# Mean of squares of a latent: one TensorE product of a summed tile instead of one per tile, issued two outputs later

## The chip, the cores and the metric

One core of one Trainium2 chip runs the whole program. TensorE (PE) multiplies matrices into PSUM banks, VectorE (DVE) and ScalarE (ACT) do elementwise work, GpSimd (POOL) a little more, and SyncE's queue (SP) issues nearly all transfers. The engines run side by side and are ordered by semaphores. The metric is the device time of one execution in microseconds; smaller is better.

## The reference, cut to what matters

```python
proj = h @ w_in                                  # 2064 rows (16 meta + 2048), width 1024
c_q, c_kv, k_rope, z = jnp.split(proj, ...)      # 384, 256, 32, 1024 columns
q = (rms_norm(c_q, q_norm_g) @ w_uq)
c_kv = rms_norm(c_kv, kv_norm_g)
k_nope = (c_kv @ w_uk); v = (c_kv @ w_uv)
# rms_norm: x * rsqrt(mean(square(x), -1) + 1e-6) * g
```

Attention, an output projection, a layer norm and a second, convolutional layer follow; the change doesn't touch them.

## The kernel before

Everything is held transposed: a latent is stored as tiles of 128 latent columns (on the partitions) by tokens. The first stage, `stage_p`, cuts the 2064 tokens into 8 chunks of 258 and makes each latent chunk by chunk. Latents 0 to 7 are the key-value ones (2 tiles of 128, `KKV`), 8 to 15 the query ones (3 tiles, `KQ`). Matrix products of float32 data are done as three products of a high and a low part (lines 43 to 45, `split_matmul`).

The order of the stage is the list `STEPS_P`: p0, p1, o0, p2, o1, p3, o2, ... p15, o14, o15, then eight z steps. Step p *g* projects chunk *g* (`project`, three tiles of 24 matmuls each into banks 0 to 2). Step o *g* makes the outputs of latent *g* (`make`): for a key-value latent 8 key tiles k0 to k7 (6 matmuls of 258 columns each) and 4 or 6 halves of value tiles v0, v1, ... (6 matmuls of 512 columns); for a query latent 12 tiles (9 matmuls each), every third of which, n = 2, 5, 8, 11, is a rotary one. Outputs go to banks 4 to 7 in turn, so output *r* waits until output *r*-4 was taken from its bank. Takers (`take`): VectorE takes the even key tiles and the rotary ones, ScalarE the rest. A key latent's step therefore has k0, k2, k4, k6 on VectorE and k1, k3, k5, k7 and all values on ScalarE.

Between the outputs of step o *g* the chain of latent *g*+1 is run, spread over three engines by hand:

- ScalarE copies the projected tiles to `craw`, VectorE squares them into `sq` (`squares`, line 588).
- TensorE's `mean_squares` (line 492) multiplies a matrix that holds 1/256 or 1/384 everywhere by each tile of `sq` in plain float32 and accumulates in bank 3. Each such product stands in the trace as two matmuls.
- VectorE adds epsilon (`mean_taken`, 614), ScalarE takes the root (390), VectorE inverts (`inverse`, 618), refines (`newton`, 621 to 624) and scales (`normalise`, 629); ScalarE rounds to the high part (394) and VectorE makes the low part (634), which raises `c_split`. Step o *g*+1 waits for that.

Pieces of weights are loaded and split into high and low parts (ScalarE 374, VectorE 581) in between: the value weights in o0, the query projection's in o2 to o4 and the `w_uq` pieces in o8.

Step o0 is special. VectorE and ScalarE first work out the sines and cosines (lines 686 to 691, 437), so k0 is taken late, and two of the three tiles of project(2) are put between its key tiles:

```python
                    make(r)
                    if n == 1 and kind == "o" and g < LAST_P:
                        mean_squares(g + 1)
                    if n == 3 and (kind, g) == ("o", 0):
                        project(2, range(KKV))
```

## Time and profile before

| | |
|---|---|
| median of 3 runs | 2629.14 us (2628.41 to 2634.87) |
| span of the profiled execution, first to last instruction | 2635.6 us |
| TensorE busy (matmul) | 2559.2 us, 97% |
| VectorE, ScalarE, GpSimd busy | 1919.0, 1447.7, 436.2 us |
| mean granted TensorE clock | 0.992 of full |
| stage_p | from 0 to about 580 us; its p and o steps end near 394 us |

The device time of the profiled execution itself isn't given; only its span is, and nothing in the profile lies around it. The span is 6.5 us above the median and within 0.8 us of the slowest of the three runs. A busy share is an average over stages; what a change is worth is read from the waits of the stage it is in.

### The profile page before, as it was taken

What the parts mean: (1) busy time and instruction counts of PE and PEld (TensorE: products, weight loads), DVE (VectorE), ACT (ScalarE), POOL (GpSimd) and SP (SyncE); (2) the same over time, 40 slices, a digit from 0 to 9 for tenths busy, and PEclk for the clock granted to TensorE, in tenths of its full rate; (3) what the DMA queues carried; (4) which work ended last, traced back from release to release, by engine and by line L of the source; (5) the groups of instructions that cost most, each with busy time, mean ns of one, the idle gap of its engine ahead of it and who ended that gap; (6) DMA issues with size and microseconds to landing.
All of it is one profiled execution on the core that took longest, in us unless ns stands there. A gap on an engine that the chain in (4) does not pass through costs nothing. (4 is left out here: it accounts for less than half of the span.)

```text
span 2635.6 us, 48070 instructions
## 1 busy us (share of the span) xinstructions
PE 2559.2 (97%) x17333; PEld 2407.8 (91%) x17333; DVE 1919.0 (73%) x3899; ACT 1447.7 (55%) x3540; POOL 436.2 (17%) x206
## 2 busy tenths in 40 slices
PE   6999999999999999999999999999999999999998
PEld 6899999999999999999999996888999999999887
DVE  5556761129999888898889886688888666666766
ACT  4433332238888888888888881124445445444310
POOL 1000000012455444444444410000000000000000
PEclk8999999999999999999999999999999999999999
DMA  4645454312233334333333316764554543553443
GB/s 150 198 147 193 146 161 131 111 47 49 51 83 82 84 84 94 86 79 75 83 75 80 77 53 174 207 205 164 207 179 170 197 157 133 180 191 136 137 146 112
DMA packets 245282, 337.06 MB, mean 128 GB/s; under 512 B 86387, under 2 KB 182531, under 8 KB 232515
## 3 DMA queue, kind: packets, MB, share of 16 engines
q1 hardware_dynamic: 227218, 325.61, 41.5%
q10 hardware_dynamic: 17840, 8.52, 1.1%
q8 instruction: 135, 2.21, 0.4%
q14 instruction: 89, 0.72, 0.1%
HBM read 224.54 MB, written 108.98 MB: 127 GB/s over the span
## 5 line engine op out<-in xcount | busy, mean ns | idle before, releaser
L1251 DVE TENSOR_TENSOR b_pt_lo<-b_transposed,b_pt_hi 128x384 fp32r<-128x384 f32 (+4 forms) x784 | 429.1, 564 | 50.2 <-ACT b_pt_hi L1148 46.8
L1148 ACT ACTIVATE b_pt_hi<-b_transposed 128x384 fp32r<-128x384 f32 (+4 forms) x784 | 382.1, 501 | 123.6 <-PE b_transposed L1182 113.9
L1135 ACT ACTIVATE ground<-b_ring,ground 128x384 f32<-128x384 f32 (+7 forms) x784 | 435.6, 560 | 19.4 <-DVE ground L1241 11.3
L1236 DVE TENSOR_REDUCE ground<-b_ring 128x1 f32<-128x384 f32 (+7 forms) x784 | 409.6, 528 | 31.8 <-PE b_ring L45 18.4
L1182 PE MATMUL b_transposed<-identity,ground 128*128 128x128 f32 (+2 forms) x2448 | 380.3, 272 | 12.0 <-DVE b_pt_lo L1251 6.5
L1199 PE MATMUL b_o_ps<-b_pt_hi,b_v 128*128 128x256 f32 (+2 forms) x1280 | 335.0, 293 | 0.7 <-DVE b_pt_lo L1251 0.7
L1182 PEld LDWEIGHTS b_transposed<-identity,ground 128*128 128x128 f32 (+2 forms) x2448 | 280.2, 135 | 60.1 <-issue 27.6
L1200 PE MATMUL b_o_ps<-b_pt_lo,b_v 128*128 128x256 f32 (+2 forms) x1280 | 313.4, 281 | 0.0
L43 PE MATMUL b_ring<-region 128*128 128x384 f32 (+7 forms) x784 | 301.5, 385 | 3.7 <-DVE b_transposed L1212 2.4
L43 PE MATMUL p_banks<-p_x_hi,big 128*128 128x258 f32 x896 | 254.5, 284 | 9.9 <-DVE big L581 8.5
L45 PE MATMUL b_ring<-region 128*128 128x384 f32 (+7 forms) x784 | 259.2, 331 | 0.0
L44 PE MATMUL b_ring<-region 128*128 128x384 f32 (+7 forms) x784 | 258.8, 330 | 0.0
L45 PE MATMUL p_banks<-p_x_hi,big 128*128 128x258 f32 x896 | 254.3, 284 | 0.0
L44 PE MATMUL p_banks<-p_x_lo,big 128*128 128x258 f32 x896 | 253.7, 283 | 0.0
L1199 PEld LDWEIGHTS b_o_ps<-b_pt_hi,b_v 128*128 128x128 f32 x1280 | 242.6, 190 | 2.6 <-DVE b_pt_lo L1251 0.9
L1200 PEld LDWEIGHTS b_o_ps<-b_pt_lo,b_v 128*128 128x128 f32 x1280 | 243.5, 190 | 0.7
L401 ACT ACTIVATE ground<-p_banks 128x258 f32<-128x258 f32 (+2 forms) x194 | 79.3, 421 | 213.1 <-PE p_banks L45 195.7
L43 PEld LDWEIGHTS p_banks<-p_x_hi,big 128*128 128x128 f32 x896 | 170.2, 190 | 10.8 <-issue 8.7
L44 PEld LDWEIGHTS p_banks<-p_x_lo,big 128*128 128x128 f32 x896 | 170.6, 190 | 0.4
L52 POOL TENSOR_TENSOR region<-ground 64x2064 fp32r<-64x2064 f32 (+1 forms) x30 | 108.7, 3624 | 372.5 <-DMA ground<-sin_queries 189.8
L45 PEld LDWEIGHTS p_banks<-p_x_hi,big 128*128 128x128 f32 x896 | 170.0, 190 | 0.0
L43 PE MATMUL p_banks<-region 128*128 128x258 f32 (+2 forms) x484 | 149.2, 308 | 19.9 <-DVE ground L646 14.4
(214 smaller groups left out, 6342.6 us busy)
## 6 DMA issues: line engine op xcount, KB each, us to landing
ground<-x_a SPq DMA_DIRECT2D x23, 1032.0 KB, 5.8
ground<-w_conv SPq DMA_DIRECT2D x32, 512.0 KB, 3.8
c_tiles<-w_conv SPq DMA_DIRECT2D x32, 512.0 KB, 4.0
c_ln<-weight_sums SPq DMA_DIRECT2D x16, 1024.0 KB, 7.8
c_tiles<-weight_sums SPq DMA_DIRECT2D x16, 1024.0 KB, 7.0
weight_sums<-c_tiles SPq DMA_DIRECT2D x9, 1024.0 KB, 3.9
keys<-ground SPq DMA_DIRECT2D x64, 129.0 KB, 5.4
queries<-ground SPq DMA_DIRECT2D x64, 129.0 KB, 2.8
```

The source lines that it names most:

```text
L43: nc.tensor.matmul(out, w_hi, x_hi, start=start, stop=False)
L44: nc.tensor.matmul(out, w_hi, x_lo, start=False, stop=False)
L45: return nc.tensor.matmul(out, w_lo, x_hi, start=False, stop=stop)
L52: return nc.gpsimd.tensor_tensor(out, x, none.to_broadcast(shape), ALU.add)
L401: nc.scalar.activation(stage_of(r, rows), bank_of(r, rows), ACT.Silu if OUTS[r][2] == "z" else ACT.Copy, scale=SCALE if OUTS[r][2] == "q" ...
L1135: nc.scalar.activation(p[0:rows, n % PSLOTS, 0:w], banks[0:rows, n % RING, 0:w], ACT.Exp, bias=nmax[0:rows, tile % 8:tile % 8 + 1], accum_ ...
L1148: nc.scalar.activation(turned(pt_hi, g, u, nb)[:, :, tile_columns(u, j)], tb[:, n % 2, 0:nb, 0:rows], ACT.Copy).then_inc(pt_hi_done, 1)
L1182: last = nc.tensor.transpose(tb[0:keys, n % 2, c, 0:rows], p[0:rows, s % PSLOTS, col:col + keys], ident[0:rows, 0:rows])
L1199: nc.tensor.matmul(ob[:, part], v[:, h % 2, vb, :], turned(pt_hi, n, u, len(blocks))[:, c, part], start=(x == 0 and c == 0), stop=False)
L1200: last = nc.tensor.matmul(ob[:, part], v[:, h % 2, vb, :], turned(pt_lo, n, u, len(blocks))[:, c, part], start=False, stop=end)
L1236: ins = nc.vector.tensor_reduce(top, bank[0:rows, 0:w], AX, ALU.max, negate=(chunks == 1))
L1251: nc.vector.tensor_tensor(lo, tb[:, n % 2, 0:nb, 0:rows], hi.bitcast(F32), ALU.subtract).then_inc(pt_split, 1)
```

## The change

`squares` adds the squared tiles to one tile on VectorE: one more add of 258 columns for a key-value latent, two for a query latent. `mean_squares` then issues a single product. It moves from behind output n = 1 to behind n = 3 of each o step. In step o0 the two tiles of project(2) move from behind n = 3 to behind n = 4. In the key-value steps VectorE takes two outputs, not one, ahead of `mean_taken`, and ScalarE takes two ahead of `root`; the later takes keep their places in the list, so each of the chain's pieces now stands behind one more take.

```diff
@@ scalar
-                    for r in mine[0:1 if keys else 2]:
+                    for r in mine[0:2]:
                         take(r)
                     if kind == "o" and g < LAST_P:
                         root(g + 1)
-                    for r in mine[1 if keys else 2:3 if keys else 4]:
+                    for r in mine[2:3 if keys else 4]:
                         take(r)
@@ tensor
             def mean_squares(g):
-                n, which = tiles_of(g), int(g >= NCA)
+                which = int(g >= NCA)
                 pe.wait_ge(squared, g + 1)
                 if g:
                     pe.wait_ge(ms_done, g)
-                for j in range(n):
-                    last = nc.tensor.matmul(banks[:, 3, 0:CA], means[:, which, :], sq[:, j, :], start=(j == 0), stop=(j == n - 1))
-                last.then_inc(mean, 1)
+                nc.tensor.matmul(banks[:, 3, 0:CA], means[:, which, :], sq[:, 0, :], start=True, stop=True).then_inc(mean, 1)
...
                     make(r)
-                    if n == 1 and kind == "o" and g < LAST_P:
+                    if n == 3 and kind == "o" and g < LAST_P:
                         mean_squares(g + 1)
-                    if n == 3 and (kind, g) == ("o", 0):
+                    if n == 4 and (kind, g) == ("o", 0):
                         project(2, range(KKV))
@@ vector, squares
-                nc.vector.tensor_tensor(sq[:, 0:n, :], craw[:, 0:n, :], craw[:, 0:n, :], ALU.mult).then_inc(squared, 1)
+                then(nc.vector.tensor_tensor(sq[:, 0:n, :], craw[:, 0:n, :], craw[:, 0:n, :], ALU.mult))
+                if n == KQ:
+                    then(nc.vector.tensor_tensor(sq[:, 0, :], sq[:, 0, :], sq[:, 2, :], ALU.add))
+                nc.vector.tensor_tensor(sq[:, 0, :], sq[:, 0, :], sq[:, 1, :], ALU.add).then_inc(squared, 1)
@@ vector, key-value steps
-                first = 1
+                first = 2
                 for r in mine[0:first]:
                     take(r)
                 if chain:
```

Line numbers of the changed file differ by one or two from those of the profile. The order of TensorE's instructions in step o0, as the difference of the two programs (`region` rows belong to key tiles, `p_x_lo` rows to a projection, `waits` names the semaphores): first the place behind the fourth key tile, k3.

```order
 L44 MATMUL p_banks<-region 128x258
 L45 MATMUL p_banks<-region 128x258
+L491 MATMUL p_banks<-ground 128x258 [waits p_ms_done,p_squared]
+L43 MATMUL p_banks<-region 128x258 [waits p_taken_dve,p_w_split]
+L44 MATMUL p_banks<-region 128x258
+L45 MATMUL p_banks<-region 128x258
+L43 MATMUL p_banks<-region 128x258
+L44 MATMUL p_banks<-region 128x258
+L45 MATMUL p_banks<-region 128x258
 L43 MATMUL p_banks<-p_x_hi,big 128x258 [waits p_c_taken,p_x_split]
 L44 MATMUL p_banks<-p_x_lo,big 128x258
```

The six matmuls of k4, with their wait for VectorE's take of k0, now stand ahead of the 48 matmuls of project(2). In the program before they stood behind them:

```order
 L44 MATMUL p_banks<-p_x_lo,big 128x258
 L45 MATMUL p_banks<-p_x_hi,big 128x258
-L43 MATMUL p_banks<-region 128x258 [waits p_taken_dve,p_w_split]
-L44 MATMUL p_banks<-region 128x258
-L45 MATMUL p_banks<-region 128x258
-L43 MATMUL p_banks<-region 128x258
-L44 MATMUL p_banks<-region 128x258
-L45 MATMUL p_banks<-region 128x258
 L43 MATMUL p_banks<-region 128x258 [waits p_taken_act,p_w_split]
```

VectorE's order in step o2 before, from the take of k0 (the COPY rows are takes of k0, k2, k4 and k6, L581 splits two pieces of weights):

```order
L646 COPY ground<-p_banks 128x258 [waits stored0,p_made]
L614 TENSOR_SCALAR ground<-p_banks 128x258 [waits p_mean]
L646 COPY ground<-p_banks 128x258 [waits stored2,p_made]
L618 RECIPROCAL ground<-ground 128x258 [waits p_rooted]
L646 COPY ground<-p_banks 128x258 [waits stored4,p_made,p_dve_step]
L581 TENSOR_TENSOR big<-ground,big 128x1024 [waits p_w_hi_done] x2
L621 TENSOR_TENSOR ground<-ground 128x258
...
L646 COPY ground<-p_banks 128x258 [waits stored6,p_made,p_dve_step]
L629 SCALAR_TENSOR_TENSOR ground<-ground 128x258 x2
```

And of the change:

```order
L647 COPY ground<-p_banks 128x258 [waits stored0,p_made]
L647 COPY ground<-p_banks 128x258 [waits stored2,p_made]
L615 TENSOR_SCALAR ground<-p_banks 128x258 [waits p_mean]
L647 COPY ground<-p_banks 128x258 [waits stored4,p_made]
L619 RECIPROCAL ground<-ground 128x258 [waits p_rooted]
L647 COPY ground<-p_banks 128x258 [waits stored6,p_made,p_dve_step]
L579 TENSOR_TENSOR big<-ground,big 128x1024 [waits p_w_hi_done] x2
L622 TENSOR_TENSOR ground<-ground 128x258
```

The take of k6 went from behind `newton` to ahead of the split of the weights. In step o0 the same list holds, with the value weights as the split pieces.

## Rows read from the trace of the kernel before

**Rows 1.** Who waited for whom, TensorE, 0 to 700 us: total, times, longest.

```profile
PE p_banks L43 <- DVE ground L646: 14.4, 4, 10.6
```

**Rows 2.** Timeline of step o3, TensorE: start, length, engine, line.

```profile
115.63 1.03 PE L492 MATMUL p_banks<-ground 128*128 128x258 f32 x4
116.62 0.28 PE L44 MATMUL p_banks<-region 128*128 128x258 f32 x1
116.74 0.28 PE L45 MATMUL p_banks<-region 128*128 128x258 f32 x1
```

**Rows 3.** Groups by line, VectorE, one addition-sized operation: count, busy, mean ns.

```profile
L621 DVE TENSOR_TENSOR ground<-ground 128x258 f32<-128x258 f32 x16 | 6.8, 425 | 0.3
```

**Rows 4.** Timeline, step o0: project(2) starts, take of k0, k4, k5.

```profile
35.46 0.28 PE L43 MATMUL p_banks<-p_x_hi,big 128*128 128x258 f32 x1
...
51.38 0.43 DVE L646 COPY ground<-p_banks 128x258 f32<-128x258 f32 x1
51.95 0.55 PE L43 MATMUL p_banks<-region 128*128 128x258 f32 x1 [10.58 <-DVE ground L646]
...
53.38 0.42 PE L43 MATMUL p_banks<-region 128*128 128x258 f32 x1
```

**Rows 5.** Timeline, step o0: take of k5, weights split low, value half v0.

```profile
54.91 0.39 ACT L401 ACTIVATE ground<-p_banks 128x258 f32<-128x258 f32 x1 [1.93 <-PE p_banks L45]
...
56.27 2.36 DVE L581 TENSOR_TENSOR region<-ground,region 128x1024 fp32r<-128x1024 f32 x2 [1.31 <-ACT region L374]
...
58.68 0.40 PE L43 MATMUL p_banks<-region 128*16 128x512 f32 x1 [1.40 <-DVE region L581]
```

**Rows 6.** Windows: busy time of each engine, granted clock (PEclk), transfers.

```profile
56.50:57.00 0.50, 0.50 (x4) 0.50 (x4) 0.50 (x1) 0.50 (x1) 0.00 (x0) 0.55 0.84 336
583.00:586.00 3.00, 1.95 (x10) 1.76 (x9) 2.85 (x10) 2.32 (x7) 0.60 (x1) 0.50 0.26 52
```

**Rows 7.** Timeline, TensorE, the idle time that stands ahead of Rows 6's second window.

```profile
581.49 0.18 PE L43 MATMUL b_ring<-region 128*16 128x16 f32 x1 [2.43 <-DVE b_transposed L1212]
```

**Rows 8.** Timeline, step o2: chain on VectorE, value half v2, take of k7, v3.

```profile
92.43 1.14 PE L492 MATMUL p_banks<-ground 128*128 128x258 f32 x4 [1.45 <-DVE ground L588]
...
94.07 0.43 DVE L646 COPY ground<-p_banks 128x258 f32<-128x258 f32 x1
...
94.85 0.28 PE L43 MATMUL p_banks<-region 128*128 128x258 f32 x1
...
101.86 0.43 DVE L646 COPY ground<-p_banks 128x258 f32<-128x258 f32 x1
...
102.34 0.50 PE L43 MATMUL p_banks<-region 128*128 128x512 f32 x1 [1.63 <-DVE ground L646]
...
103.65 1.11 ACT L401 ACTIVATE ground<-p_banks 128x258 f32<-128x258 f32 x2
...
104.07 0.50 PE L43 MATMUL p_banks<-region 128*128 128x512 f32 x1
```

**Rows 9.** Timeline, step o7: VectorE's take of k0.

```profile
203.82 0.43 DVE L646 COPY ground<-p_banks 128x258 f32<-128x258 f32 x1
```

**Rows 10.** Timeline, step o8: last pieces of w_uq, output n = 4.

```profile
231.37 1.04 ACT L374 ACTIVATE region<-ground 128x384 fp32r<-128x384 f32 x2 [1.44 <-DMA ground<-w_uq]
...
232.83 0.36 PE L43 MATMUL p_banks<-region 128*128 128x258 f32 x1 [1.31 <-ACT ground L401]
```

**Rows 11.** Timeline, step o10: first output, mean taken, n = 2 and n = 5 taken, n = 9.

```profile
273.53 0.28 PE L43 MATMUL p_banks<-region 128*128 128x258 f32 x1
...
277.20 0.43 DVE L614 TENSOR_SCALAR ground<-p_banks 128x258 f32<-128x258 f32 x1 [2.08 <-PE p_banks L492]
...
278.28 1.74 DVE L643 TENSOR_TENSOR ground<-p_banks,ground 64x258 f32<-64x258 f32 x4 [0.65 <-PE p_banks L45]
...
281.85 1.74 DVE L643 TENSOR_TENSOR ground<-p_banks,ground 64x258 f32<-64x258 f32 x4
...
284.56 0.28 PE L43 MATMUL p_banks<-region 128*128 128x258 f32 x1
```

## The prediction

> **What bounds the kernel now.** I read the page first: TensorE is busy 97% of the span, so a microsecond counts when TensorE loses or gains it. Then the list of who waited for whom on TensorE over the first 700 us, because the change lies in that stretch: nearly all of the stage's waiting is for VectorE's takes of key tiles [rows 1], 14.4 us in four waits, of which one alone is 10.6. Then the timeline of the o steps, engine by engine. It shows three kinds of step. In o3 to o6 and o9 to o13 TensorE runs through its key or query tiles without idle time in the place of the mean. In o1, o2, o7 and o8 VectorE or the weight pieces are late and TensorE waits near the mean in any case. In o0 it stands still until k0 is taken.
>
> **What a product costs.** The four matmuls of one mean (two products) push the next ones from 115.63 to 116.74 us, in which two ordinary ones of 0.12 us also start [rows 2]: (1.11 - 0.24) / 4 = 0.2175 us each, 0.435 us a product. The change takes out one product in 8 means and two in 8 others, 24 in all: 24 x 0.435 = **10.4 us** at most. The adds cost 0.425 us each in an operation of their size [rows 3], about 0.46 with the hand-over between dependent ones: 8 x 1 + 8 x 2 = 24 adds, 11 us of VectorE's time. What counts is where each lands.
>
> **The start (project(1)).** Latent 0's chain comes 0.4 us earlier and its squares 0.46 later through the add; both meet in VectorE's angle work, which fixes the take of k0. I count 0.
>
> **Step o0, the large term.** Before, k3 is followed by 48 matmuls of project(2), which start at 35.46 and fill 5.8 us of the time in which VectorE and ScalarE make the sines. Then TensorE idles 10.58 us until k0's take at 51.38 frees k4's bank at 51.95 [rows 4]. The difference of the two programs shows k4, with its wait for k0's take, moved ahead of these 48 matmuls. So they no longer fill the idle time: TensorE idles from about 35 to 51.95, does k4 until 53.38 [rows 4], and only then the projection. Behind it k5 comes late; ScalarE's take of k5 stands ahead of its split of the value weights, that ahead of VectorE's low part, and v0 waits for that [rows 5]. From the take of k5 to v0 the chain needs 58.68 - 54.91 = 3.77 us, before and now (VectorE's take of k6, which now stands ahead of its split, is done by then).
> When is k5 made? The granted clock was half from the long idle time until 56.95: the window 56.5 to 57 has a mean of 0.55 [rows 6]. At half the clock a matmul takes (53.38 - 51.95) / 6 or, without the first one's start, 0.215 us. From 53.38 to 56.95 go 16.6 of the 48, the other 31.4 take 31.4 x 0.12 = 3.8 us: 60.7. k5 takes 0.72, its take comes 0.2 later: 61.6, where it was at 54.91. Step o0 costs **+6.7 us**. Bounds: were the clock full again at once, 48 x 0.12 = 5.8 and a faster k5 give +5.1; were it half throughout, 48 x 0.215 = 10.3 and a slow k5 give +10.1. I take 6.7, by the window that this trace has.
>
> **A clock term.** v0 now stands behind an idle time of its own: k7 ends near 63.0, v0 comes at 58.68 + 6.7 = 65.4, so 2.4 us. The nearest row is an idle time of 2.43 us at 581.49 [rows 7], and the clock was at 0.50 in the window behind it [rows 6]; the idle times of 1.63 and 1.65 us in o2 and o3 had no such consequence. A stretch of 3.4 us at half the clock costs 1.7. I give it 6 in 10: **+1.0 us** in the sum, 0 to 3.4 as bounds.
>
> **Steps o1 and o2.** In o2 the mean waited 1.45 us for the squares [rows 8], which end at 92.38. VectorE then turns the rotary key and takes k0 at 94.07, and k4 starts at 94.85. Now the add puts k0's take 0.46 later, to end at 94.96, so k4 starts at 95.0: the mean's product lies wholly in a wait for VectorE and its saving is lost. Behind it the chain goes on with mean taken, k4's take, reciprocal, k6's take, weights, refining. Before, v2 waited 1.63 us for k6's take at 101.86, which stood behind the refining [rows 8]. That wait goes. But v3 needs k7's bank, and ScalarE takes k7 at 103.65 behind the latent's high part; v3 started at 104.07 right behind it [rows 8]. So the wait only moves one output on, and what counts is k7's take. Its chain begins about 1.0 us later (mean taken behind one more take, 0.33, and the add, 0.46, reciprocal behind k4 that is made late) and saves 0.34 at k6 and 0.33 at idle time ahead of the weights: I get +0.3 at v3. The same reckoning in o1 gives +0.3 at k4. The transfers of o1's keys, on which ScalarE's value takes wait, leave 0.46 later, which adds 0.2 in o2. Together **+0.8 us**.
>
> **Steps o3 to o6.** VectorE has idle time ahead of k0's take, so the add is hidden there, and the product's 0.435 us is real. In o3 and o4 v2's wait of the same kind goes (two of the four of rows 1) and v3's for k7 takes its place; since reciprocal, k6 and refining lie close behind the shortened mean, k7's take comes 0.4 earlier too. 4 x 0.42 = **-1.7 us**. If the cover of k7 failed in o5 and o6, where it has 0.1 to 0.2 us to spare, half of it is lost.
>
> **Step o7.** The mean of latent 8 has three tiles, two adds, and one table scaling of 1.23 us stands between them and k0's take. That take ends at 203.82 + 0.43 + 0.92 = 205.17 [rows 9] and k4 waits for it, at 205.25 where it was 205.53. Then k7's take comes 0.8 later and v3 waits. **+0.3 us**, where -0.87 stood to be won.
>
> **Step o8.** n = 4 started at 232.83 behind ScalarE's take, which stood behind the last `w_uq` pieces at 231.37, which waited for their transfer [rows 10]. That transfer waits for VectorE to free the slot, and VectorE does so behind the squares of latent 9. Two adds put it off by 2 x 0.46: **+0.9 us**, and the mean's saving lies in this wait.
>
> **Steps o9 to o13.** From the first output's start (273.53) mean taken began 3.67 us later, n = 9 began at 11.03 [rows 11]. Now the product ends at 4 x 1.08 + 0.435 = 4.755, mean taken starts 0.2 later at 4.96. On VectorE two rotary takes and the reciprocal follow: 281.85 + 1.74 - 277.20 - 0.65 of idle time = 5.74 to the end of n = 5's take [rows 11]. Output 9 needs its bank: 4.96 + 5.74 + 0.05 = 10.75. So each step wins 11.03 - 10.75 = 0.28, not 0.87: a third. 5 x 0.28 = **-1.4 us**. Bounds: -0.87 x 5 = -4.4 and, if each take's hand-over costs 0.15 more, -0.6.
>
> **Step o14.** No projection follows it; o15 waits for the low part directly. The chain's rotary take starts at 5.30 behind the first output where it was 4.75: **+0.5 us**.
>
> **Sum.** 6.7 + 1.0 + 0.8 - 1.7 + 0.3 + 0.9 - 1.4 + 0.5 = **+7.1 us**. Everything behind 394 us runs the same orders later. The profiled execution's span is 2635.6 us, with nothing shown around it, so the sum against it is 2642.7; it lies 6.5 above the median of the runs, and I carry the difference to the median: 2629.1 + 7.1 = **2636.2 us**.
>
> **Rivals.**
> *Almost nothing (0 to +5 us).* The projection is exposed less, because the clock comes back sooner (+5.1 for o0), no drop at v0 and o9 to o13 win all of 4.4: 5.1 + 0.8 - 1.7 + 0.3 + 0.9 - 4.4 + 0.5 = +1.5. For it: these are all bounds of rows. Against: it needs them together; one or two give +4. Chance 0.3, time 2633.
> *Slow: the clock.* v0's idle time drops the clock for 6.8 us (3.4 lost), and the projection runs longer at half: +10 to +12, 2640. For it: the row at 583; against: the gaps of 1.6 us passed. Chance 0.2.
> *Faster: TensorE is the bound and sheds work.* If no output waits for VectorE behind the shorter mean and o0's k4 found its bank free, TensorE wins 10.4 us, and with v2's three waits of 1.65, 1.63 and 0.5 gone 14.2: 2615 to 2619. It decides once VectorE's takes run over 1 us ahead of TensorE's needs. Against it stand the 14.4 us of [rows 1] and the bank that k4 needs. Chance 0.04. In the Trainium skill, Perfetto Trace Analysis, Identifying Performance Opportunities says to improve the most-contended engine, the one with the highest occupancy, first, and by that rule moving work from TensorE to VectorE gains about 10 us; the trace's waits speak against it here.
> The forecast's own case (+5 to +9.5) has 0.46.
>
> **How the numbers follow.** A change under 0.3% (7.9 us) is about what a measurement of this kernel can't tell from none. The forecast's case straddles that: 0.31 of its 0.46 lie within, 0.15 above. Within: 0.31 + 0.29 = 0.60; slower: 0.15 + 0.20 + 0.01 = 0.36; faster 0.04. The range leaves out the faster rival and the end of the slow one: 2630.5 to 2640.5.
>
> **What the changed profile would show.** (1) TensorE idle from about 35 to 51.9 us in one wait of 16 to 17 us for VectorE's take, and the 48 projection matmuls behind 53 us. (2) v0 of o0 near 65.4 us. (3) In o2 no wait at v2, one at v3. (4) 32 matmuls on the mean's line, not 80. (5) Query steps about 22.6 us long, not 22.9, with small gaps at n = 6 and n = 9. (6) o8's n = 4 about 0.9 later in its step. Wrong would be: v0 before 62, or query steps shorter by 0.8.

## The result: 15 us slower, where 7 were forecast

| | median | runs |
|---|---|---|
| kernel before | 2631.97 us (2628.41 to 2634.87) | 5, three of them those of the table of before |
| changed kernel | 2647.01 us (2641.03 to 2650.85) | 6 |

The ratio is 1.0058, with a 95% interval of 1.0048 to 1.0068: 12.6 to 17.9 us slower, 15.3 in the middle. This lies above the forecast's range, whose end was 2640.5. A sixth run of before that took 4169 us is left out.

### The profile of the changed kernel

The span of its profiled execution is 2645.8 us, where it was 2635.6; the mean granted clock is 0.988, where it was 0.992. TensorE has 48 records less. Its own matmul time is hardly smaller, because it ran longer at half its clock. The spans differ by 10.2 us and not by 15 because the stretch behind the first stage was 4.6 us longer in the profiled execution of before (2054.1 us, and 2049.5 in this one). The page's first part:

```profile
span 2645.8 us, 47997 instructions
PE 2558.4 (97%) x17285; PEld 2403.8 (91%) x17285; DVE 1927.5 (73%) x3923; ACT 1447.1 (55%) x3540; POOL 436.5 (16%) x206
```

Who waited for whom on TensorE in the first 700 us, the counterpart of [rows 1] (columns: line that waits, releaser, total, times, longest):

```profile
PE p_banks L43 <- DVE ground L647: 20.8, 4, 17.3
...
PE p_banks L43 <- ACT ground L401: 7.0, 5, 3.2
PE p_banks L43 <- DVE region L635: 3.3, 2, 2.3
...
PE p_banks L491 <- DVE ground L589: 2.0, 2, 1.8
```

Waits for VectorE's takes of key tiles went from 14.4 to 20.8 us, waits for ScalarE's takes (L401) from 1.5 to 7.0 in five places, the waits for a latent's low part (L635) from 2.5 to 3.3.

To see where the time went, I cut the stage at the first matmul of each step in the trace of TensorE. The lengths in us, worked out from these starts ("to o1" is from the span's start to the first matmul of step o1; a p step is 8.6 to 8.7 where not named):

| | before | changed | forecast of the difference | measured |
|---|---|---|---|---|
| to o1 | 67.1 | 75.2 | +7.7 | +8.0 |
| o1 | 13.6 | 13.9 | +0.3 | +0.3 |
| o2 | 16.2 | 19.0 | +0.5 | +2.8 |
| o3 and p5 | 23.1 | 24.3 | -0.4 | +1.2 |
| o4, o5, o6, each | 13.4, 12.3, 12.2 | 13.0, 11.8, 11.8 | -0.4 | -0.4 |
| o7 | 15.7 | 16.2 | +0.3 | +0.4 |
| o8 | 16.6 | 19.4 | +0.9 | +2.8 |
| o9 to o13, each | 14.25 | 13.95 | -0.28 | -0.3 |
| o14 and o15 | 28.9 | 30.9 | +0.5 | +2.0 |
| end of stage_p | 581.5 | 596.3 | +7.1 | +14.8 |

Four places make the error: o2, o3 with p5, o8, and o14 with o15. In the other steps the working holds to a few tenths. This is one execution; a second one of the same program, further down, has a shorter stage.

*Step o0*, the timeline of TensorE and of the two engines that it waits for (columns: start, length, engine, line, operation, tiles, and the idle time ahead with its releaser); it answers to [rows 4, 5]:

```profile
51.96 0.55 PE L43 MATMUL p_banks<-region 128*128 128x258 f32 x1 [17.27 <-DVE ground L647]
...
53.38 0.42 PE L43 MATMUL p_banks<-p_x_hi,big 128*128 128x258 f32 x1
...
61.37 0.39 ACT L401 ACTIVATE ground<-p_banks 128x258 f32<-128x258 f32 x1 [8.38 <-PE p_banks L45]
...
62.73 2.36 DVE L579 TENSOR_TENSOR region<-ground,region 128x1024 fp32r<-128x1024 f32 x2
...
65.15 0.40 PE L43 MATMUL p_banks<-region 128*16 128x512 f32 x1 [2.37 <-DVE region L579]
```

k4 starts at the same 51.96, the projection behind it, k5's take at 61.37 (forecast 61.6) and v0 at 65.15 (forecast 65.4).

*Step o2.* The same columns. ScalarE's value take of step o1 waits for the key stores of o1, then come the split of the next x, VectorE's low part, the squares, and TensorE:

```profile
93.38 0.60 ACT L401 ACTIVATE ground<-p_banks 128x512 f32<-128x512 f32 x1 [5.87 <-DMA keys<-ground]
...
97.18 1.92 ACT L362 ACTIVATE p_x_hi<-ground 128x2064 fp32r<-128x2064 f32 x1
...
102.08 0.43 DVE L589 TENSOR_TENSOR ground<-ground 128x258 f32<-128x258 f32 x1
...
102.57 0.70 PE L491 MATMUL p_banks<-ground 128*128 128x258 f32 x2 [1.77 <-DVE ground L589]
104.68 0.58 PE L43 MATMUL p_banks<-region 128*128 128x258 f32 x1 [1.41 <-DVE ground L647]
```

*Steps o3, o8 and o15*, the first matmul behind each wait:

```profile
137.92 0.58 PE L43 MATMUL p_banks<-region 128*128 128x512 f32 x1 [2.04 <-ACT ground L401]
...
245.14 0.55 PE L43 MATMUL p_banks<-region 128*128 128x258 f32 x1 [3.24 <-ACT ground L401]
...
394.59 0.58 PE L43 MATMUL p_banks<-region 128*128 128x258 f32 x1 [2.27 <-DVE region L635]
```

And the windows around them (columns: window, its length, busy time and count of PE, PEld, DVE, ACT, POOL, granted clock, DMA share, GB/s):

```profile
60.00:104.00 44.00, 37.53 (x244) 31.92 (x242) 21.39 (x35) 15.90 (x29) 0.00 (x0) 0.96 0.41 132
104.00:110.00 6.00, 5.32 (x24) 5.32 (x25) 4.35 (x8) 2.95 (x5) 0.00 (x0) 0.51 0.64 203
110.00:136.00 26.00, 25.42 (x165) 22.72 (x164) 16.80 (x27) 9.46 (x16) 0.00 (x0) 0.98 0.56 176
136.00:144.00 8.00, 6.08 (x32) 5.52 (x33) 2.48 (x5) 5.11 (x7) 0.00 (x0) 0.79 0.77 273
144.00:240.00 96.00, 94.05 (x670) 87.79 (x670) 54.55 (x88) 37.71 (x71) 0.00 (x0) 1.00 0.50 160
240.00:252.00 12.00, 8.76 (x51) 8.38 (x50) 9.16 (x19) 3.90 (x10) 0.00 (x0) 0.72 0.55 188
252.00:390.00 138.00, 137.54 (x1113) 134.73 (x1113) 104.90 (x185) 44.60 (x88) 0.00 (x0) 1.00 0.48 159
390.00:400.00 10.00, 7.73 (x53) 7.52 (x52) 6.56 (x15) 2.17 (x5) 0.00 (x0) 0.83 0.50 148
```

This table shows the pattern of the error in this execution: the clock is full or nearly so wherever no wait stood, and behind each of the four waits it is at the lower of its two levels (1.2 GHz) for part of a window. A clock of 0.51 over 6 us costs nearly 3 us of work; the 0.72 over 12 us is 3.4 us, of which a part falls into the idle time and costs nothing.

### The profile page after: what moved, and what is told of

It is laid out like the page before. It is cut to its first block and busy times, and to the rows that moved or that the text cites. A ratio compares the mean times of both kernels' runs of the same rounds, so it can differ in the third digit from the quotient of the medians.

```text
span 2645.8 us, 47997 instructions
## 1 busy us (share of the span) xinstructions
PE 2558.4 (97%) x17285; PEld 2403.8 (91%) x17285; DVE 1927.5 (73%) x3923; ACT 1447.1 (55%) x3540; POOL 436.5 (16%) x206
## 5 line engine op out<-in xcount | busy, mean ns | idle before, releaser
L1136 ACT ACTIVATE ground<-b_ring,ground 128x384 f32<-128x384 f32 (+7 forms) x784 | 436.3, 561 | 19.4 <-DVE ground L1242 11.2
L1237 DVE TENSOR_REDUCE ground<-b_ring 128x1 f32<-128x384 f32 (+7 forms) x784 | 409.6, 528 | 31.4 <-PE b_ring L45 15.3
L401 ACT ACTIVATE ground<-p_banks 128x258 f32<-128x258 f32 (+2 forms) x194 | 78.7, 421 | 215.0 <-PE p_banks L45 199.6
L43 PE MATMUL p_banks<-region 128*128 128x258 f32 (+2 forms) x484 | 153.3, 317 | 33.9 <-DVE ground L647 20.8
```

The lines of the kernel that those rows point to most:

```text
L43: nc.tensor.matmul(out, w_hi, x_hi, start=start, stop=False)
L1136: nc.scalar.activation(p[0:rows, n % PSLOTS, 0:w], banks[0:rows, n % RING, 0:w], ACT.Exp, bias=nmax[0:rows, tile % 8:tile % 8 + 1], accum_ ...
L1237: ins = nc.vector.tensor_reduce(top, bank[0:rows, 0:w], AX, ALU.max, negate=(chunks == 1))
```

## The experiments

Every session timed the kernel before again, and its medians differ a little: 2630.31, 2629.7, 2633.51 and 2629.9 us, each on another chip. So each kernel is compared with the runs of its own session.

### One part of the change at a time

**Projection back.** The changed kernel with project(2) behind k3 again:

```diff
-                    if n == 4 and (kind, g) == ("o", 0):
+                    if n == 3 and (kind, g) == ("o", 0):
                         project(2, range(KKV))
```

> The whole change, but the two tiles of project(2) stand behind output n = 3 of step o0 again, ahead of k4. Theory A (the exposed projection is the main cost: it lost 8.0 us in step o0 and the rest came from its late clock and the steps behind it): 9 to 13 us below the changed kernel, so -1 to +4 us against the kernel before; TensorE's idle time ahead of k4 is about 10 us again and v0 comes near 59 us. Rival B (the adds on VectorE and the later mean are the main cost, through late takes and late transfers in o1, o2 and o8): still +7 us or more against the kernel before.

2638.35 us, ratio 1.0026 [1.0015, 1.0037]: 6.8 us above before and 8.4 below the changed kernel. "To o1" is 67.2 us again. The bound that I gave for the remaining parts (at most +4) fell: they cost 6.8. o1 takes 16.9 us now, o2 17.5, o14 and o15 29.6. The 8.4 us are not the projection's price alone: o1 is 3.0 us longer than in the changed kernel, with two waits (1.86 and 1.42 us) and 3.4 us of half clock in it, and the step behind o0 is 8.0 us earlier.

**Projection only.** The kernel before with project(2) behind k4:

```diff
-                    if n == 3 and (kind, g) == ("o", 0):
+                    if n == 4 and (kind, g) == ("o", 0):
```

> The kernel before with this one part: the two tiles of project(2) moved from behind n = 3 to behind n = 4 of step o0. Nothing else. Theory A: +8 to +12 us against the kernel before. By my own term for step o0 +6.7, with 1.0 of clock at most +7.7. Rival B: +7 at most, and the steps o2 and o8 keep their lengths of 24.8 and 25.3 us (outputs and projection).

2637.06 us, ratio 1.0022 [1.0013, 1.0031]: +5.8 by the ratio, +6.8 by the medians. In its timeline:

```profile
51.59 0.55 PE L43 MATMUL p_banks<-region 128*128 128x258 f32 x1 [16.32 <-DVE ground L646]
...
64.81 0.41 PE L43 MATMUL p_banks<-region 128*16 128x512 f32 x1 [2.37 <-DVE region L581]
```

The mechanism of the large term stands, and so does its size within 0.6 us: v0 comes 6.1 us later (forecast 6.7), and "to o1" is 73.2. The clock term (+1.0) is not seen here: the wait ahead of v0 is the same 2.37 us as in the changed kernel, but the granted clock stays full behind it. No later step changes by over 0.5 us.

**Sum only.** The kernel before with the adds and the single product, everything else in its old place:

```diff
-                for j in range(n):
-                    last = nc.tensor.matmul(banks[:, 3, 0:CA], means[:, which, :], sq[:, j, :], start=(j == 0), stop=(j == n - 1))
-                last.then_inc(mean, 1)
+                nc.tensor.matmul(banks[:, 3, 0:CA], means[:, which, :], sq[:, 0, :], start=True, stop=True).then_inc(mean, 1)
...
+                if n == KQ:
+                    then(nc.vector.tensor_tensor(sq[:, 0, :], sq[:, 0, :], sq[:, 2, :], ALU.add))
+                nc.vector.tensor_tensor(sq[:, 0, :], sq[:, 0, :], sq[:, 1, :], ALU.add).then_inc(squared, 1)
```

> The kernel before with this one part: VectorE adds the squares and the mean takes one product, at its old place behind n = 1, all takes in their old order. Theory A: -1 to -4 us against the kernel before: 0.44 each in o3 to o6 and 0.44 in each query step (the product is 0.87 shorter, but the two adds end 0.4 after n = 1), against +0.9 or more in o8. Rival B: slower than before by 3 us or more, since the adds alone make takes and transfers late.

2635.39 us, ratio 1.0014 [1.0005, 1.0023]: 1.3 to 6.0 us slower, where a gain was expected. Steps o3 to o7 and o9 to o14 behave (o3 14.0, o5 11.8, o9 13.8 us); the loss is 0.5 in o1, 2.6 in o2 and 1.8 in o8. "To o1" is 68.2, which is 1.1 above the first execution of before but inside what that kernel does by itself (66.6 to 68.9 in four executions). In o2 the mean waits, and the clock is at 0.79 in the 8 us around it:

```profile
95.50 0.70 PE L491 MATMUL p_banks<-ground 128*128 128x258 f32 x2 [3.02 <-DVE ground L589]
```

The window:

```profile
92.00:100.00 8.00, 4.98 (x27) 4.72 (x27) 7.22 (x10) 2.07 (x7) 0.00 (x0) 0.79 0.16 27
```

**Placement only.** The kernel before with the mean behind n = 3 and two takes ahead of the chain's pieces, but with a product per tile:

```diff
-                    for r in mine[0:1 if keys else 2]:
+                    for r in mine[0:2]:
...
-                    for r in mine[1 if keys else 2:3 if keys else 4]:
+                    for r in mine[2:3 if keys else 4]:
...
-                    if n == 1 and kind == "o" and g < LAST_P:
+                    if n == 3 and kind == "o" and g < LAST_P:
...
-                first = 1
+                first = 2
```

> The kernel before with this one part: the mean stands behind n = 3 and the key steps take two outputs ahead of the chain's pieces; two or three products as before, no adds, project(2) at its old place. Theory A, by the chain of the query steps: mean taken starts 4.32 + 1.305 + 0.2 = 5.83 us behind the first output, n = 9 at 5.83 + 5.79 = 11.6 where it was 11.03: +0.6 in each of five steps, +3 us, and 0 to +1 in the key steps. Rival B: +5 or more.

2638.34 us, ratio 1.0031 [1.0022, 1.004]: +8.2, twice what was expected. The part that was reckoned is there: o9 to o13 take 14.85 us each, +0.6. What was not reckoned: v3 of o2 waits for k7's take, p4 behind it takes 10.1 us and not 8.6, o3 with p5 24.7, o8 18.5, and o14 with o15 31.9:

```profile
105.48 0.50 PE L43 MATMUL p_banks<-region 128*128 128x512 f32 x1 [2.04 <-ACT ground L401]
...
392.31 0.40 PE L43 MATMUL p_banks<-region 128*128 128x258 f32 x1 [2.29 <-DVE region L634]
```

The window around the second:

```profile
380.00:400.00 20.00, 17.65 (x127) 16.95 (x126) 14.42 (x30) 4.72 (x12) 0.00 (x0) 0.91 0.48 144
```

Sum alone (+3.7) and placement alone (+8.2) together make +6.8, not +11.9: in the query steps the shorter product pays for a part of the later place.

### Is it the clock, the transfers, or the waits alone?

**Fillers in the idle places.** The changed kernel with 60 small matmuls, whose results go unused, into a free bank at the places where TensorE waits (ahead of v0 in o0, and in o1, o2, o3, o8, o15):

```diff
+            FILL = {(0, 8): 10, (1, 4): 5, (2, "mean"): 7, (2, 4): 6, (3, 11): 9, (8, 4): 15, (15, 0): 8}
...
+                for _ in range(FILL[at]):
+                    nc.tensor.matmul(banks[:, 0 if at[0] else 4, 0:P], means[:, 0, :], means[:, 0, :], start=True, stop=True)
```

> The whole change, with 60 extra float32 products of 128 columns (0.22 us each, results unused, into a free bank) set into the places where TensorE idles in the changed kernel: 10 ahead of v0 of o0, 5 ahead of k4 of o1, 7 ahead of the mean and 6 ahead of k4 of o2, 9 ahead of v3 of o3, 15 ahead of n = 4 of o8, 8 ahead of o15. Theory C (idle times of 2 us and more make the chip grant half the clock, and that, not the waits alone, is what my sum missed): in spite of 13 us more work it is 3 to 9 us below the changed kernel, and the granted clock from 60 to 410 us is 1.00 where it was 0.97. Rival D (the waits themselves are the loss, the clock only coincides): the same as the changed kernel or up to 5 us slower.

The window that stood at 0.51 is at full clock, and so is all from 69.5 to 410 us. For comparison the windows' row of the changed kernel:

```profile
60.00:410.00 350.00, 332.44 (x2424) 313.90 (x2423) 225.51 (x387) 125.58 (x237) 0.00 (x0) 0.97 0.50 161
```

And of the kernel with fillers:

```profile
104.00:110.00 6.00, 6.00 (x48) 5.77 (x47) 5.03 (x10) 3.58 (x7) 0.00 (x0) 1.00 0.51 146
...
60.00:410.00 350.00, 342.09 (x2587) 325.73 (x2587) 228.70 (x391) 125.39 (x237) 0.00 (x0) 1.00 0.51 163
```

o2 falls from 19.0 to 17.0 us, o3 from 15.1 to 14.1, o8 from 19.4 to 16.8, o14 with o15 from 30.9 to 29.4: 7.1 us over the four places that were off. But "to o1" rose by 2.1, because the fillers of o0 missed their place. They ran behind the wait and not in it, put v0 off to 68.25, and the clock fell all the same (0.72 from 64 to 70 us):

```profile
64.90 3.69 PE L550 MATMUL p_banks<-ground 128*128 128x128 f32 x20 [2.37 <-DVE region L597]
```

The whole took 2644.73 us (5 runs), ratio to before 1.0058 [1.0045, 1.0072], the same as the changed kernel's ratio. Measured against the second execution of the changed kernel, in which o3 and o15 were short without any filler, the fillers save 1.9 us in o2 and 1.0 in o8 and nothing elsewhere. So this experiment alone does not settle what the clock costs.

**The same wait with and without the half clock.** The traces at hand settle more. In several of them the same wait stands at the same place, and only the clock behind it differs. Here is v3 of o3 in the second execution of the changed kernel, to be set beside the 2.04 us and the 0.79 above:

```profile
137.07 0.50 PE L43 MATMUL p_banks<-region 128*128 128x512 f32 x1 [2.04 <-ACT ground L401]
...
136.00:144.00 8.00, 6.93 (x52) 6.67 (x53) 2.44 (x3) 5.27 (x8) 0.00 (x0) 1.00 0.67 236
```

| place and wait | clock fell behind it | clock stayed full | kernel before | forecast of the difference |
|---|---|---|---|---|
| v3 of o3, 2.04 us: o3 and p5 | changed, first execution: 24.3 | changed, second: 22.7 | 23.1 | -0.4 |
| first output of o15, 2.27 to 2.29 us: o14 and o15 | changed, first: 30.9 | changed, second: 29.4; projection back, loads late, latent 9: 29.6 | 28.9 | +0.5 |
| n = 4 of o8: o8 | changed, first (3.24 us): 19.4; second (2.65 us): 17.8 | projection back (2.48 us): 16.6 | 16.6 | +0.9 |

Where the clock stays full, o3 and o15 come out as the forecast had them; where it falls, each costs 1.5 us more for the same wait. The waits of o8 are not of one length, but there too the step without the fall is no longer than before. So in o3 and o15 the missed cost is the half clock (Theory C), and in o8, as far as unequal waits can be compared, most of it. Whether it comes behind a wait of 2.0 to 2.5 us differs from one execution of the same program to the next. The timed runs agree: the two fastest of the changed kernel's six have a mean granted clock of 0.991, the four slower ones 0.987 to 0.989. Their mean is 0.9892, where the kernel before has 0.9927 to 0.9933 in its four sessions. The difference is 9 to 11 us of the whole at most, since half the clock in idle time costs nothing.

**Loads late.** The changed kernel with the two w_x loads of step o1 issued behind the key stores, not between them:

```diff
-                    if n < LOADS_AT.get((kind, g), 0) and g != LAST_P:
+                    if 0 <= n - (8 if g == 1 else 0) < LOADS_AT.get((kind, g), 0) and g != LAST_P:
```

> The whole change, but the two weight pieces that SyncE's queue loads between the key stores of o1 stand behind its first two value stores. Theory E (the late key stores of o1, held up behind x and weight transfers, delay ScalarE's value takes and through them the squares of latent 3): v0's take in o1 comes 15 us or less behind the step's start where it is 18.2, o2 shortens from 19.0 to 16 to 17.5 us, 1 to 3 us off the whole. Rival F (the takes are late for the chain's sake): no change in o1 and o2.

2644.12 us (4 runs), ratio 1.0058 [1.0043, 1.0074]: not told apart from the changed kernel. In the trace the value take that waits for the key stores starts 17.1 us behind the start of o1, where it is 18.2 in the changed kernel and 15.1 before:

```profile
91.24 0.60 ACT L401 ACTIVATE ground<-p_banks 128x512 f32<-128x512 f32 x1 [4.71 <-DMA keys<-ground]
```

o2 takes 16.0 us, but p4 and p5 take 9.8 and 9.6. The loads are about a third of the delay, 1.1 us of 3.1, and the time returns behind it. Neither theory holds as it was put: the take was to come at 15 us or less by E, and not to move by F.

**Latent 9 with three products.** The changed kernel with the old squares and products for this one latent:

```diff
+        summed_tiles = lambda g: g != NCA + 1
...
+                n = 1 if summed_tiles(g) else tiles_of(g)
```

> The whole change, but latent 9's mean keeps its three products and has no adds. My term: o8 was +0.9 through the adds ahead of the w_uq pieces, so o8 goes from 19.4 to near 17 us (16.7 before). If the adds are the cause of the 3.2 us wait at n = 4, that wait is 1.3 to 2.3 us and 1 to 3 us come off the whole; if they are not, the wait stays above 3.

o8 takes 15.8 us, not 19.4, and the wait at its n = 4 is 0.78 us:

```profile
242.91 0.36 PE L43 MATMUL p_banks<-region 128*128 128x258 f32 x1 [0.78 <-ACT ground L402]
```

2643.06 us (4 runs), ratio 1.0052 [1.0036, 1.0067]. With the two adds ahead of the release of the `w_uq` slot this wait is 2.27 to 3.24 us in five traces; without them it is 0.6 to 1.7 in four executions of the kernel before. So in the changed kernel the adds cause it. They are not the only way to it: the placement-only kernel has no adds and waits 2.40 us there. The price against the changed kernel's two executions is 3.6 and 2.0 us, not the 0.9 of the adds: the wait grew from 1.31 [rows 10] to 3.24 and 2.65, and the clock fell. What the whole gains from it, 1.6 us by the ratios, is less than the intervals can tell.

**Latents 2 and 3 alone.** The kernel before, with the sum for these two latents and nothing else:

```diff
+        summed_tiles = lambda g: g in (2, 3)
```

> The kernel before with the sum for latents 2 and 3 alone, the means at their old place. Two adds and two products less, no other edit. If late squares and late transfers of o1 and o2 are what made the sum alone 5 us slower (o2 was 18.8 us in it), this is +2 to +4 us, with o2 at 18 us or more and half the clock in it. If the loss was in o8 and elsewhere, it is within 1 us of the kernel before.

2638.22 us, ratio 1.0016 [1.0007, 1.0025]: two adds of 0.43 us make the kernel 4.2 us slower, as much as the sum in all 16 latents. Two steps differ from before: o1 takes 14.05 us where it took 13.6, and o2 19.0 where it took 16.2 to 16.5 in four executions. ("To o1" is 68.8, which the kernel before reaches by itself.) The two adds stand in these two steps; which of them costs how much is not separated. Here the chain can be followed row by row. SyncE's queue (SPq: length of the issuing, x for how many) in step o1, in the kernel before:

```profile
73.14 1.94 SPq L266 DMA_DIRECT2D ground<-x_a  x1
75.13 0.44 SPq L279 DMA_DIRECT2D keys<-ground  x1
75.61 0.43 SPq L262 DMA_DIRECT2D ground<-w_x  x1
76.09 0.81 SPq L279 DMA_DIRECT2D keys<-ground  x1
76.94 0.44 SPq L262 DMA_DIRECT2D ground<-w_x  x1
77.43 3.27 SPq L279 DMA_DIRECT2D keys<-ground  x6
```

And in this kernel:

```profile
75.30 0.58 SPq L267 DMA_DIRECT2D ground<-x_a  x1
75.93 1.42 SPq L280 DMA_DIRECT2D keys<-ground  x1
77.39 1.39 SPq L263 DMA_DIRECT2D ground<-w_x  x1
78.82 1.44 SPq L280 DMA_DIRECT2D keys<-ground  x1
80.31 0.43 SPq L263 DMA_DIRECT2D ground<-w_x  x1
80.78 3.60 SPq L280 DMA_DIRECT2D keys<-ground  x6
```

The last key store is issued at 80.70 and 84.38, that is 13.6 and 15.6 us behind the start of o1. The add of 0.43 us is not simply carried along: counted from the start of o1 the first store's issuing begins earlier than before (7.1 us, where it was 8.0) and ends at nearly the same time (8.5). The 2 us come behind it: the next load and the next store take 1.39 and 1.44 us to issue, where they took 0.43 and 0.81, and the last six stores 3.60, where they took 3.27. Ahead of them the issuing of the x load is shorter (0.58 us, where it was 1.94). The last store is 15.5 to 15.7 us behind the start of o1 in this trace, in the sum-only one and in both of the changed kernel, and 13.5 to 13.7 in all four of before. Long issues alone don't lengthen o2, though: the projection-only kernel has no add, shows issues of 1.24 and 1.35 us there and its last store at 14.6, and its o2 takes 16.1. Why the issuing slows is open. The take that waits for these stores comes 1.6 and 2.6 us later. In the timeline of ScalarE before:

```profile
82.25 0.60 ACT L401 ACTIVATE ground<-p_banks 128x512 f32<-128x512 f32 x1 [3.49 <-DMA keys<-ground]
```

And here:

```profile
86.99 0.60 ACT L402 ACTIVATE ground<-p_banks 128x512 f32<-128x512 f32 x1 [6.06 <-DMA keys<-ground]
```

So it stands 15.1 and 18.2 us behind the start of o1, 3 us later with an add of 0.43. In o2 the mean waits 3.20 us and the clock falls. The window of the kernel before:

```profile
95.00:100.00 5.00, 5.00 (x35) 4.60 (x34) 4.48 (x5) 2.83 (x5) 0.00 (x0) 1.00 0.77 236
```

TensorE's row of this kernel, and its window:

```profile
96.34 1.18 PE L494 MATMUL p_banks<-ground 128*128 128x258 f32 x2 [3.20 <-DVE ground L596]
```

```profile
95.00:100.00 5.00, 3.66 (x16) 3.47 (x17) 4.33 (x10) 1.10 (x3) 0.00 (x0) 0.66 0.31 36
```

### Was the profiled execution typical?

> The kernel before once more, for its trace. If the execution that the prediction was built on was a typical one, its steps have the same lengths (o1 13.6, o2 16.2, o8 16.6, o14 and o15 28.9 us) and the first stage ends at 581.5 us. If it was a slow one, as its clock of 0.992 against a mean of 0.993 in 44 executions says, the stage ends 3 to 5 us earlier, and part of what I read as waits of the kernel is that execution's own.

> The kernel before a third time, to see how its steps vary: o1, o2, o3 and o8, in which VectorE or a transfer is waited for, by 0.5 us or more; o4 to o6 and o9 to o13 by less than 0.1.

> The kernel before on the same chip, for the length of its stages beside the selective one: the first stage 581 us, all behind it 2051 us. Under H the selective kernel's stretch behind the first stage is 4 us or more longer than this one's; under G it is the same within 2.

> The changed kernel once more. If its long steps are its own, o2 is 18 us or more, o8 18 us or more, o14 and o15 together 30 us or more again, with half the clock in each; if they belong to the execution profiled, at least two of the three are within 0.5 us of the kernel before.

| execution | time | to o1 | o2 | o8 | o14 and o15 | stage's end | behind it |
|---|---|---|---|---|---|---|---|
| before, of the prediction | | 67.1 | 16.2 | 16.6 | 28.9 | 581.5 | 2054.1 |
| before, second | 2634.12 | 66.6 | 16.5 | 16.7 | 29.0 | 581.5 | 2050.8 |
| before, third | 2633.79 | 67.1 | 16.4 | 15.7 | 28.9 | 580.7 | 2051.3 |
| before, fourth | 2635.49 | 68.9 | 16.2 | 16.5 | 29.0 | 583.3 | 2050.4 |
| changed, first | 2647.55 | 75.2 | 19.0 | 19.4 | 30.9 | 596.3 | 2049.5 |
| changed, second | 2649.39 | 74.4 | 18.9 | 17.8 | 29.4 | 591.0 | 2056.6 |

The step lengths that the forecast rested on were typical. o1, o3, o4 to o6 and o9 to o13 repeat within 0.1 us, o2 within 0.3, o8 within 1.1; of the steps that were expected to vary by 0.5 or more, only o8 does. In the fourth execution of before the wait ahead of v0 was 2.34 us, where it had been 1.40, and the clock fell there as it did in the changed kernel. Every timed execution on record lasts 1.8 us longer than its span, so the execution of the prediction took about 2637.4 us, an estimate, which is some 8 us and not 6.5 above the median that it was set beside. The forecast carried only the difference over, so it isn't touched by that.

Neither outcome that was set for the changed kernel came: o2 (18.9 us) is as long again, o8 (17.8) and o14 with o15 (29.4) are in between, o3 (14.1) is short. In this execution the stage is 9.5 us longer than before, 2.4 more than forecast, and nearly all of that is o2. Yet it was no faster as a whole: the stretch behind the stage, whose program is unchanged, took 2056.6 us. That stretch varies from 2044.3 us (placement only) to 2056.6 over all traces, and what makes it vary is open. So o2's loss belongs to the kernel, o8's in part; those of o3 and o15 come and go with the clock; and how the 15.3 us divide between the stage and the rest in a typical execution is not shown.

### The parts that win, alone

**Selective.** The kernel before with the sum only for latents 5 to 7 and 10 to 15, the mean behind n = 3 in o4 to o6 and behind n = 2 in the query steps from o9:

```diff
+        summed_tiles = lambda g: 5 <= g < NCA or g > NCA + 1
+        late_mean = lambda g: 4 <= g < NCA - 1
...
+                    if n == (3 if late_mean(g) else 2 if g > NCA else 1) and kind == "o" and g < LAST_P:
```

> The sum only where the profile has it hidden: latents 5 to 7 and 10 to 15, and the mean behind n = 3 with two takes ahead only in o4 to o6, behind n = 2 in o9 to o14; everything else, project(2) too, as in the kernel before. By the rows: 3 x 0.42 in o4 to o6, 5 x 0.87 in o9 to o13 (the mean taken is 0.2 later, and n = 6 and n = 9 keep their banks free) and 0.5 ahead of o15: -6 us against the kernel before, -3 to -8. If the adds cost wherever they stand: 0 or slower.

> The same kernel as the selective one once more. Its first stage was 7.6 us shorter than that of the kernel before in the profile, but its median only 0.8. Theory G (the saving is real and the median of 11 runs was off through the clock of the later stages): -4 us or more against the kernel before. Rival H (the saving is given back behind the stage in most executions): within 2 us again.

**Queries only.** As above with `summed_tiles` only for g > NCA + 1 and no late mean in the key steps.

> The kernel before with the sum for latents 10 to 15 alone and their mean behind n = 2; no key step touched, so nothing ahead of 245 us differs. Theory G: each of o9 to o13 0.9 us shorter and 0.5 ahead of o15: -5 us. Rival H: within 2 us of the kernel before.

The steps do what was expected: o9 to o13 take 13.3 to 13.4 us each, 0.9 less, which is the two products of 0.435 us each; o4 to o6 in the first kernel win 0.4 each. The profiled spans are 2624.6, 2627.6 and 2630.2, where those of before lie between 2632.0 and 2635.6. But the timed medians are those of before: 2628.95 with a ratio of 0.9998 [0.9989, 1.0007], 2629.38 with 0.9997 [0.9988, 1.0006], and 2631.04 with 1.0003 [0.9994, 1.0012]. A gain of 6 us (0.23%) lies outside all three intervals.

The stages of the three profiles end at 573.9, 577.8 and 577.0 us, 3 to 9 us earlier than in any execution of before, and the stretches behind them (2050.8, 2049.8 and 2053.2 us) are not longer than before. But these profiled executions are themselves timed ones, of 2626.40, 2629.38 and 2632.02 us, on chips where the kernel before has medians of 2629.7 and 2629.9. The spans of before that they were set beside come mostly from elsewhere: on the chip of the second and third executions its median is 2633.51, and the fourth, 2635.49 us, is slower than all 21 timed ones on its chip. Compared on the same chip, the three are 3.3 us below, 0.5 below and 2.1 above the median of before. The timed executions also show a lower mean granted clock: 0.9919, 0.9918 and 0.9912, where before has 0.9933, 0.9929 and 0.9929. That is worth 3 to 4.5 us of the whole at most, half and more of what is missing of the gain. One place is seen: the wait ahead of o15 is 1.80 us in all three, where it was 1.46, and in one of them the clock fell there and o14 with o15 took 30.0 us. The other places are open.

## Why the prediction was wrong

Point by point, by what it said the changed profile would show:

1. **One wait of 16 to 17 us in o0: right** (17.27, till 51.96; the projection from 53.38).
2. **v0 near 65.4: right** (65.15). "To o1" grew by 8.0, forecast 7.7 with the clock term. The clock term happened in this execution (0.72 in the window from 64 to 70 us). It had been given 6 in 10, and it doesn't come every time: in the changed kernel's second execution and in the projection-only kernel the clock stayed full behind the same wait of 2.37 us. Moved alone, the projection costs 5.8 to 6.8 us of the whole and 6.1 in the step.
3. **In o2 no wait at v2, one at v3: the shift was right, the size was not.** The placement-only kernel has it (2.04 us). In the changed kernel the mean's and k4's waits (1.77 and 1.41) are the larger ones and v3's is 0.45.
4. **32 matmuls on the mean's line: right.**
5. **Query steps shorter by a third of the saving: right**, 0.3 each and o4 to o6 by 0.4 each.
6. **o8's n = 4 0.9 us later: right, the step was not.** n = 4 starts 8.16 us behind the start of the step, where it was 7.40, and 7.56 in the second execution. That the adds ahead of the release of the weight slot lengthen the wait was shown by latent 9 with three products. But the step lost 2.8 and 1.2 us in these two executions, in which the clock fell behind the wait, and nothing where it didn't.

**The step that failed** stands in the part on o1 and o2: "The transfers of o1's keys, on which ScalarE's value takes wait, leave 0.46 later, which adds 0.2 in o2." The kernel with latents 2 and 3 alone showed in its place 3 us in the takes and 2.8 us in o2, and that this one spot is as large as the whole sum-only loss. I had given the transfers a price of their delay, without following SyncE's queue, in which two loads of w_x stand between the key stores. These loads are 1.1 of the 3.1 us; the rest lies in the issuing of the stores and their landing, and why it is slower stays open.

**The second failed step** is the same in o3, o8 and o14: every wait was priced at its own length. I had allowed one clock term, at v0, because the idle times of 1.6 us in the trace before had no consequence and the one of 2.43 had. I didn't ask which other waits the change would lift from 1.3 or 1.6 to over 2: o8's (1.31 to 3.24), v3's in o3 (2.04), o15's (2.27). The same waits without the half clock behind them leave o3 and o15 where the forecast had them (-0.4 and +0.5), and with it each is 1.5 us longer. The fall is not certain behind such a wait, so a term with a chance of its own at each of these places would have been the right form. For the time of the whole, the mean clocks of the timed runs allow it up to 9 to 11 us; its exact share was not shown. The length of a fall differs too: the forecast took 3.4 us, which came behind v0, in o3 and in o15, but in o2 and o8 the half clock lasted 6.8 us.

Of the rivals, the slow one (the clock, +10 to +12, chance 0.2) was nearest, but it placed the clock's loss at v0 and in the projection, where it was no larger than forecast. The Trainium skill's rule (Perfetto Trace Analysis, Identifying the Most-Contended Engine) is to optimise the engine with the highest occupancy first. Read as it was in the prediction, it stands for a gain of 10 us, an estimate from the 24 products fewer [rows 2]; the measured time went the other way by 15, though TensorE was busy 97% of the span.

## What to carry to other kernels

Work that leaves the busiest engine is won only in the steps where that engine waits for nothing; here 24 x 0.435 us left TensorE, and 8 steps of the stage won 0.3 to 0.4 us each, while in the first execution four places lost 1 to 3. Before an operation is put ahead of a point on which transfers wait, follow the queue that issues them to its last transfer and to whoever waits for it, not only to the first. And where a change lengthens a wait of TensorE, look for rows of longer waits in the same trace and at the clock behind them, and price the wait with that stretch, for each place and not once, and with a chance, since the clock does not fall every time. Before a long step is called the change's, look at a second execution, and compare times on the same chip.

## What was unexpected of the hardware

- Two VectorE adds of 0.43 us each made the kernel 4.2 us slower [1.8 to 6.6]. In its trace the last key store is issued 2.0 us later, the take that waits for the stores comes 3.0 us later, the mean waits 3.20 us, and the clock falls.
- Two idle times close together were followed by half the clock: 1.77 and 1.41 us within 4 us in o2, then a clock of 0.51 from 104 to 110 us, and likewise 1.71 and 1.41 us in the second execution. One of 1.63 us by itself in the kernel before [rows 8] was not.
- Behind the same wait the clock fell in one execution and not in another: 2.04 us ahead of v3 of o3 (0.79 and 1.00 over 8 us), 2.27 and 2.29 us ahead of o15. A wait of 2.48 us in o8 passed at full clock, one of 2.40 didn't.
- The same program's o3 took 15.1 and 14.1 us, and its o14 with o15 30.9 and 29.4, in two executions.
- Three kernels whose profiled spans were 2 to 11 us shorter than those of the kernel before had its timed median within 1.2 us. The spans were compared across chips, and the stage that became shorter came with a lower mean clock in the timed runs.
